# Expert weights in transfers of two neighbouring chunks (16 KB for a partition), one semaphore for both

## What is computed

```
def moe_ffn(h, w_router, b_router, w_gu, b_gu, w_down, b_down):
    logits = (hf @ w_router) + b_router
    top_val, top_idx = lax.top_k(logits, TOP_K)        # 4 of 32 experts for each token
    gates = jax.nn.softmax(top_val, axis=-1)
    ...
    def run_block(args):                               # rows of one expert
        tok, gate, e = args
        gu = hf[tok] @ w_gu[e] + b_gu[e]               # 1024 -> 2048
        gt = jnp.minimum(gu[:, :D_FF], SWIGLU_LIMIT)
        up = jnp.clip(gu[:, D_FF:], -SWIGLU_LIMIT, SWIGLU_LIMIT)
        act = (up + 1) * (gt * jax.nn.sigmoid(SWIGLU_ALPHA * gt))
        return (act @ w_down[e] + b_down[e]) * gate[:, None]      # 1024 -> 1024
```

## Time and profile before

| | us |
|---|---|
| median of 3 runs | 1410.5 |
| lowest and highest | 1408.39, 1412.58 |
| the profiled execution's own time | 1413.6 |
| its span, first to last instruction | 1411.8 |
| TensorE busy | 1297.4 (92%) |
| VectorE busy | 952.5 (67%) |
| ScalarE busy | 602.2 (43%) |

### The profile page before, as it was taken

The page is one execution under the profiler, slowest core; times in us unless marked ns, Lnnn a source line. Parts: engine busy times, 40 slices in busy tenths (PEclk is TensorE's granted clock), DMA queues, the critical chain, the costliest instruction groups (busy, mean ns, idle before and its releaser), DMA issues.

```text
span 1411.8 us, 25062 instructions
## 1 busy us (share of the span) xinstructions
PE 1297.4 (92%) x6265; PEld 531.3 (38%) x6265; DVE 952.5 (67%) x1576; ACT 602.2 (43%) x636; POOL 220.7 (16%) x149
## 2 busy tenths in 40 slices
PE   4699869879999999999999999999999989999993
PEld 2487437723332333333333333333323323333330
DVE  2899899766666666656666656666666656666654
ACT  3332762443534444334444444444425344444434
POOL 1732144011011110101111111101010111111110
PEclk9799979979999999999999999999999999999997
DMA  9675231689999999994999999999999962999995
GB/s 378 223 243 179 105 142 60 243 309 389 407 403 397 420 397 404 407 399 170 390 405 399 410 394 411 397 415 401 405 403 398 404 241 71 384 404 389 403 397 216
DMA packets 87780, 473.29 MB, mean 335 GB/s; under 512 B 14289, under 2 KB 14801, under 8 KB 37585
## 3 DMA queue, kind: packets, MB, share of 16 engines
q1 hardware_dynamic: 76930, 454.17, 80.5%
q0 software_dynamic: 10832, 18.90, 5.8%
HBM read 462.00 MB, written 18.35 MB: 340 GB/s over the span
## 4 chain that ended last, share of the span: by engine, by line
PE 57%; DMA 18%; SPq 9%; DVE 6%; ACT 5%; issue 3%; POOL 2%; DVEq 1%; ACTq 0%; POOLq 0%
PE ps L1490 29%; DMA ring<-in_w_down 16%; PE ps L1502 14%; SPq L321 8%; ACT window L745 3%; PE ps L1482 2%; DMA wm<-in_w_mod 2%; PE ps L1285 2%; PE ps L1286 2%; PE ps L1287 2%; PE ps L1512 1%; PE ps L1472 1%; DVE catR_lo L976 1%; PE ps L1325 1%; DVE Um L936 1%
## 5 line engine op out<-in xcount | busy, mean ns | idle before, releaser
L1490 PE MATMUL ps<-window,xT 128*64 128x512 f32 x2880 | 642.2, 598 | 6.3 <-ACT window L745 6.0
L1002 DVE COPY window<-ring 128x2048 f32 x360 | 438.0, 1225 | 215.4 <-PE ps L1490 109.2
L1502 PE MATMUL ps<-window,aT 128*64 128x512 f32 x1440 | 333.0, 600 | 17.9 <-DVE window L1002 12.5
L1490 PEld LDWEIGHTS ps<-window,xT 128*64 128x64 f32 x2880 | 198.3, 137 | 395.7 <-issue 365.8
L745 ACT ACTIVATE window<-ring 128x2048 f32 x180 | 340.0, 1908 | 10.8 <-DMA ring<-in_w_down 4.7
L739 ACT ACTIVATE sg<-gb 128x256 f32<-128x256 f32 x90 | 37.5, 416 | 574.9 <-DVE gb L1171 574.9
L552 POOL DMA_INDIRECT out_parts<-osb,idx_c x46 | 81.7, 1775 | 800.5 <-DVE osb L1220 783.9
L1502 PEld LDWEIGHTS ps<-window,aT 128*64 128x64 f32 x1440 | 94.0, 136 | 214.4 <-issue 145.0
L1171 DVE TENSOR_SCALAR gb<-ps 128x256 f32<-128x256 f32 x90 | 38.1, 424 | 111.6 <-PE ps L1490 111.4
L537 POOL DMA_INDIRECT xg<-h_rows,idx_n x46 | 45.0, 979 | 228.4 <-DVE idx_n L1049 177.1
L752 ACT ACT_TABLE_LOAD x45 | 57.7, 1283 | 7.0 <-issue 6.2
(11 more groups left out here) (297 smaller groups left out, 1107.1 us busy)
## 6 DMA issues: line engine op xcount, KB each, us to landing
ring<-in_w_gate_up SPq DMA_DIRECT2D x256, 1024.0 KB, 21.7
ring<-in_w_down SPq DMA_DIRECT2D x128, 1024.0 KB, 23.7
wm<-in_w_mod SPq DMA_DIRECT2D x4, 2048.0 KB, 21.7
wm_a<-in_w_mod SPq DMA_DIRECT2D x4, 2048.0 KB, 9.2
wm_b<-in_w_mod SPq DMA_DIRECT2D x4, 2048.0 KB, 8.9
win<-in_w_in SPq DMA_DIRECT2D x3, 2048.0 KB, 20.1
x_in<-in_x SPq DMA_DIRECT2D x1, 2048.0 KB, 10.7
wo_f<-in_w_out SPq DMA_DIRECT2D x1, 2048.0 KB, 7.3
```

The source lines that it names most:

```text
L1002: V.tensor_copy(window[c % NW][:, :, :, :], ring_chunk(c, p)).then_inc(S["moved_a"], 1)
L1490: last = MMUL(ps[M * j:M * (j + 1), h, :].rearrange("m (g n) -> m g n", g=2), xT[:, k, :], window[c % NW][:, k % CK, :, j * GW:(j + 1) * G ...
L1502: last = MMUL(ps[M * y:M * (y + 1), 2, :], aT[:, h, i, M * j:M * (j + 1)], window[c % NW][:, k % CK, y, :], start=False, stop=(h == 1 and ...
```

## The change

A transfer now carries two neighbouring chunks: 128 partitions of 16 KB, 2 MiB, laid out in memory as one contiguous block with 16 KB for each partition. The layout on chip is unchanged: two neighbouring slots of the ring hold the two chunks. There are 6 transfers for an expert in place of 12, and one semaphore for each pair. SP waits, before it issues a pair, until the second chunk of the two whose slots it takes has been moved. The copies into the windows stay one chunk each, in the same order; both chunks of a pair now wait for the pair's semaphore.

```
-        w_ld = [sem(f"w_loaded_{c}") for c in range(NCH)]
-        def load_chunk(sp, c, e, p):
-            s = bass.ds((p * NCH + c) & (NR - 1), 1)
-            src = wgu[e, c, :, :] if c < NGU else wd[e, c - NGU, :, :]
-            sp.dma_start(ring[:, s, :, :, :].rearrange("p s k g n -> p (s k g n)"), src).then_inc(w_ld[c], 16)
+        w_ld = [sem(f"w_loaded_{c}") for c in range(NCH // 2)]
+        def load_two(sp, c, e, p):
+            s = bass.ds((p * (NCH // 2) + c // 2) & (NR // 2 - 1), 1)
+            src = wgu[e, c // 2, :, :] if c < NGU else wd[e, (c - NGU) // 2, :, :]
+            two = ring.rearrange("p (s d) k g n -> p s (d k g n)", d=2)
+            sp.dma_start(two[:, s, :].rearrange("p s n -> p (s n)"), src).then_inc(w_ld[c // 2], 16)
...
-                for c in range(NCH):
+                for c in range(0, NCH, 2):
                     if c >= NR - NCH:
-                        wait_moved(sp, c - (NR - NCH), ahead)
+                        wait_moved(sp, c + 1 - (NR - NCH), ahead)
                     elif ahead_of_last is not None:
-                        wait_moved(sp, c + 2 * NCH - NR, ahead_of_last)
+                        wait_moved(sp, c + 1 + 2 * NCH - NR, ahead_of_last)
                     sp.nop(nofuse=True)
-                    sp.wait_ge(w_ld[c], 16 * i)
+                    sp.wait_ge(w_ld[c // 2], 16 * i)
                     sp.nop(nofuse=True)
-                    load_chunk(sp, c, e, i)
+                    load_two(sp, c, e, i)
...
             def move(c, p, b):
-                act.wait_ge(w_ld[c], 16 * p + 16)
+                act.wait_ge(w_ld[c // 2], 16 * p + 16)
...
+def in_twos(chunks):
+    v = chunks.reshape(NE, -1, 2, P, chunks.shape[3]).transpose(0, 1, 3, 2, 4)
+    return np.ascontiguousarray(v).reshape(NE, v.shape[1], P, -1)
```

More of the change, by code:

```diff
@@ L417, in _ @@
             sp.wait_ge(S["pf_done"], TL)
-            load_chunk(sp, 6, 0, 0)
-            load_chunk(sp, 7, 0, 0)
+            load_two(sp, 6, 0, 0)
             store_h(0)
@@ L422, in _ @@
             sp.wait_ge(S["pr_done"], TL)
-            for c in range(4):
-                load_chunk(sp, c, 0, 0)
+            load_two(sp, 0, 0, 0)
+            load_two(sp, 2, 0, 0)
             store_h(2)
             store_h(3)
-            load_chunk(sp, 4, 0, 0)
-            load_chunk(sp, 5, 0, 0)
+            load_two(sp, 4, 0, 0)
             sp.wait_ge(S["lg_done"], TL)
-            load_chunk(sp, 10, 0, 0)
-            load_chunk(sp, 11, 0, 0)
+            load_two(sp, 10, 0, 0)
             sp.wait_ge(S["h_stored"], 16 * TL)
             sp.wait_ge(S["gathered"], 16)
-            load_chunk(sp, 8, 0, 0)
-            load_chunk(sp, 9, 0, 0)
+            load_two(sp, 8, 0, 0)
             sp.wait_ge(S["table_ready"], 1)
@@ L729, in _ @@
             for c in range(NW):
-                act.wait_ge(w_ld[c], 16)
+                act.wait_ge(w_ld[c // 2], 16)
                 A(window[c][:, :, :, :], ring_chunk(c, 0), ACT.Copy).then_inc(S["moved_a"], 1)
@@ L1000, in move @@
             def move(c, p):
-                dve.wait_ge(w_ld[c], 16 * p + 16)
+                dve.wait_ge(w_ld[c // 2], 16 * p + 16)
                 V.tensor_copy(window[c % NW][:, :, :, :], ring_chunk(c, p)).then_inc(S["moved_a"], 1)
@@ L1546, in expert_biases @@
     return np.ascontiguousarray(np.concatenate([rows, rows]))
+def in_twos(chunks):
+    v = chunks.reshape(NE, -1, 2, P, chunks.shape[3]).transpose(0, 1, 3, 2, 4)
+    return np.ascontiguousarray(v).reshape(NE, v.shape[1], P, -1)
 def gate_up_chunks(w):
     v = np.asarray(w)[0].reshape(NE, NGU // 2, CK, P, 2, 2, HF)
-    return np.ascontiguousarray(v.transpose(0, 5, 1, 3, 2, 4, 6)).reshape(NE, NGU, P, CK * 2 * HF)
+    return in_twos(v.transpose(0, 5, 1, 3, 2, 4, 6).reshape(NE, NGU, P, CK * 2 * HF))
 def down_chunks(w):
     v = np.asarray(w)[0].reshape(NE, NCH - NGU, CK, P, D)
-    return np.ascontiguousarray(v.transpose(0, 1, 3, 2, 4)).reshape(NE, NCH - NGU, P, CK * D)
+    return in_twos(v.transpose(0, 1, 3, 2, 4).reshape(NE, NCH - NGU, P, CK * D))
 def kernel(x, c, ctx, c_ctx, w_mod, b_mod, g_norm_mix, g_norm_ffn, w_in, w_fourier, conv_w,
```

## The result

| | us |
|---|---|
| before, median of 6 runs | 1410.99 (1408.39 to 1412.58) |
| after, median of 6 runs | 1421.81 (1417.82 to 1422.09) |
| ratio, with its 95% interval | 1.0075 (1.0061 to 1.0089) |

The change makes the kernel slower by 10.8 us. The forecast was 1411, so no change, with 1407 to 1415 of its own: that is missed. 1422 lies inside the stated range of 1399 to 1427 only because the range took in the first rival.

The account below looks back on a forecast made before the run. DMA was taken to bound three streams, so only their starts, chunk time and ends count. 7.8 + 7.4 - 15.3 + 0.5 = +0.4 us, put at 1411 us on a median of 1410.5; range 1399 to 1427.

Parts of the forecast that it names:

- first rival: Weight transfers: rows cost by the byte or are cut in two, so term 3 is zero; 1426 us, chance 0.22.
- What bounds the kernel: Three long stretches (streams), 991 of 1411.8 us, are bound by DMA; work on TensorE, VectorE or ScalarE is absorbed there.
- Term 1: Three stream starts: SP waits for the second move, so each starts one chunk, 2.6 us, later; +7.8 us.
- Term 2: Three stream ends: move 10 waits for chunk 11's landing, so move 11 comes 2.47 us later; +7.4 us.
- Term 4: GpSimd's gathers, delayed by longer weight rows: only the very first gather's reader waits beyond its cover; +0.5 us.
- Term 3: Weight transfers in a full queue: 16 KB rows save 42 ns for each of 367 chunks; -15.3 us.
- upper bound: Term 3's far end: the rate rises from 421 to the fastest window's 434 GB/s, saving 28 us.
- third rival: The late gather: weight rows twice as long delay every gather and TensorE waits; up to 1529 us, chance 0.08.

Follow-up runs that it names:

- pairs_8k: Kernel before with issue and landing both paired, still in 1 MiB transfers with 8 KB rows: 1421.48 us, ratio 1.0076.
- late_issue: Kernel before, but SP issues two chunks behind one wait, the later one; transfers and semaphores stay single: 1414.76 us, ratio 1.0031.
- late_landing: Kernel before, but the two transfers of a pair count up one semaphore and every move waits for both: 1418.11 us, ratio 1.0046.
- light_quiet_8k: light_8k with the index bounds of gathers and scatter-adds set to 0, so they move next to nothing: 1317.76 us, ratio 0.9337.
- light_quiet pair: light_quiet_8k, and the changed kernel (16 KB rows) with the same matmuls left out and the same quiet gathers and scatter-adds: 1317.76 and 1305.37 us.
- mixed: Changed kernel, but chunks 4, 5, 10 and 11 are single transfers with their own semaphores, in 8 KB rows: 1418.49 us, ratio 1.0054.
- light_gather_8k: light_8k with the scatter-adds quiet and the gathers at work: 1369.67 us, ratio 0.9729.
- light_8k: pairs_8k with the first of two k steps of every chunk left out of the expert matmuls: 1408.57 us, ratio 0.9982.

## Why the prediction was right or wrong

- **What bounds the kernel: right.** Half of the experts' matmuls gone took 0.9% off the time of pairs_8k, and nothing off its streams.
- **Term 1, the starts, +7.8: right in kind, too large.** late_issue alone costs 4.4 us. The old start had gaps, so a later one loses less.
- **Term 2, the ends, +7.4: right.** 6.5 us in late_landing; the moves are 2.08 us apart where I used 2.47.
- **Term 4, the gather's reader, +0.5: next to nothing.** The landing went where it was expected, 10.1 us, and stayed covered in the loop; the reader of the first gather waited 0.5 us in place of 0.3.
- **Term 3, the time of a chunk, -15.3: this is the step that failed.** Forecast -15.3, measured 0 with an uncertainty of 3 (pairs_8k against after). I wrote that no row shows a queue of 16 KB rows and bounded it by row lengths, from "nothing" to 28 us. The line itself held: 429 GB/s in a quiet window, -12.4 us where the gathers and scatter-adds move nothing. What it left out is that "full windows" were all windows without a gather. (The 434 of the upper bound was no pure row length either: 96 of its 173 packets are under 8 KB and 19 are completions.) The streams run at 394 to 403, and the 20 GB/s between that and 421 are the gathers and scatter-adds, since light_quiet_8k has 420 for a whole stream; I multiplied the saving by all 367 chunks as if that share stayed as it was. It grew by about as much as the rows saved.

With the measured terms the sum is 4.4 + 6.5 + 0 + 0 = 10.9 us, against the measured 10.8. The two terms are uncertain by 1.5 and 2 us, so that they agree to 0.1 is chance. The forecast missed by 11 us and not by 15 because two errors of opposite sign met: terms 1 and 2 were 4 us too large together, and term 3 promised 15 us that did not come.

The first rival foretold the time, 1426 with term 3 at zero, but for another reason (rows cost by the byte, or are cut in two), and that reason is refuted by the light_quiet pair and by the packet counts. The third rival had the mechanism, weight rows that delay the gather, and looked only at who waits for the gather's data. The Trainium skill (DMA: Bandwidth & Descriptors, "Queues, rings and completion order"), by which an engine takes turns packet by packet, was cited there; the gather's landing at 6.8, 7.5 and 10.1 us for rows of 4, 8 and 16 KB agrees with it, though no run shows the turns themselves. Its fixed 2.0 us for each transfer ("Anatomy of one DMA"), which that section gives for transfers issued from GpSimd and not from SyncE, does not add up in a full queue here: with 192 transfers fewer, after is no faster than pairs_8k.

Open is why a weight packet takes longer beside the packets of a gather. In the dip the engines are busy (a mean share of 0.99 or more, though 0.90 in one row above) while they move up to a quarter less, so it isn't that they stand idle. What slows the packets, and why 16 KB is so much worse than 8 KB, no run here tells.

## What to carry to other kernels

When a stretch is bound by DMA, compare its mean rate with that of its quiet windows first. What lay between here was taken by the gathers and scatter-adds, and the change of the weight rows changed that part as well: a price found in quiet windows held only for quiet windows. A transfer that is merged makes its first half wait for its second at every place where the queue runs empty or somebody stands behind it: here 11 us for three starts and three ends, and in mixed, freeing the last pair shifted the wait to the pair before.

## What was not expected of the hardware

- A gather costs the stream of weights far more than its own bytes. One gather is up to 64 rows of 4 KB and moves 0.18 MB on average (10.55 - 2.19 MB for 46 of them, by the pages of light_gather_8k and light_quiet_8k), 0.43 us at 421 GB/s. The rate of a window counts these bytes too, and by the table above the dip costs light_gather_8k (421 - 395) x 12 / 421 = 0.74 us more. That makes 1.2 us. The run times say the same: with gathers and scatter-adds quiet the light kernel is 91 us shorter (ratio 0.9982 to 0.9337), and 36 us with the scatter-adds alone quiet (to 0.9729), so some 1.2 us for each of the 45 gathers, and 0.8 for each scatter-add.
- The scatter-adds land later too: the median goes from 9.0 us (pairs_8k) to 11.3 (after), though nothing in the loop waits for it.
- TensorE's granted clock fell when its work was halved: the mean is 0.97 in the kernel before and 0.83 in light_8k. Two neighbouring windows of light_gather_8k:

```profile
720.97:722.97 2.00, 0.76 (x3) 0.30 (x4) 0.00 (x0) 2.00 (x2) 0.00 (x0) 0.82 1.02 426
722.97:724.97 2.00, 2.00 (x6) 0.30 (x4) 0.00 (x0) 1.33 (x2) 0.00 (x0) 0.50 1.00 301
```

In the second the clock is 0.50, the 1.2 GHz level; it fell within the first, in which TensorE was busy for 0.76 of 2.00 us. The mean matmul on the gate and up weights takes 721 ns in light_8k and 598 in the kernel before. That is why leaving out half of the matmuls took TensorE's busy share only from 0.97 (306.18 of 316 us) to 0.72 (202.06 of 280) in a window of light_8k:

```profile
320.00:600.00 280.00, 202.06 (x766) 54.84 (x762) 174.89 (x311) 117.07 (x114) 31.02 (x24) 0.84 1.02 402
```
